# Prompt attention: the gathered value rows of the sample's sparse branch moved from the last tiles of sparse heads to the tiles ahead of them

## The reference, cut to what matters

```python
idx = indexer_topk(q_i, w_i, pos, ik_all, topk)
v_sel = gather_selected(pool_v.astype(v_b.dtype), page_table, v_b, idx, past_len)
dsa_o = dsa_attend(q_b, pos, k_sel, v_sel, idx)

def dsa_attend(q, q_pos, k_sel, v_sel, idx):
    ...
    p = jax.nn.softmax(s, axis=-1).astype(v_sel.dtype)
    o = jnp.einsum('bhqs,bqshd->bqhd', p, v_sel)
```

## Time and profile before

| what | before |
|---|---|
| median of 3 runs | 1791.02 us (1786.36 to 1791.84) |
| the profiled execution | 1787.65 us, span 1785.7 us |
| PE busy | 1640.2 us (92% of the span) |
| DVE busy | 867.5 us (49%) |
| ACT busy | 424.1 us (24%) |
| POOL busy | 345.0 us (19%) |

### The profile page before, as it was taken

How to read it: one execution, slowest core, us unless ns; L and a number is a source line. 1 busy time by engine, 2 the same in 40 slices (tenths; PEclk the granted TensorE clock), 3 DMA queues, 4 the chain that set the end, 5 groups by cost and what they waited for, 6 DMA issues and landing times.

```text
span 1785.7 us, 21665 instructions
## 1 busy us (share of the span) xinstructions
PE 1640.2 (92%) x8572; PEld 1008.0 (56%) x8572; DVE 867.5 (49%) x1636; ACT 424.1 (24%) x1111; POOL 345.0 (19%) x348
## 2 busy tenths in 40 slices
PE   6999989999989899977687699989999999989998
PEld 3644545447766666655453466535777777754443
DVE  3447897995805677774778633222222222210011
ACT  2132221010015455443355432001111111100000
POOL 2100000010006677761445520000000000000000
PEclk9899989999999899997788899999999999999999
DMA  8311221143217788776445744502212212112100
GB/s 259 131 48 63 100 76 61 68 183 112 92 67 254 267 284 261 270 235 194 138 131 151 240 140 155 153 0 80 73 48 71 71 48 77 65 36 71 63 23 31
DMA packets 89846, 218.38 MB, mean 122 GB/s; under 512 B 13576, under 2 KB 37520, under 8 KB 83696
## 3 DMA queue, kind: packets, MB, share of 16 engines
q0 software_dynamic: 29168, 116.66, 20.1%
q1 hardware_dynamic: 59506, 93.24, 15.8%
q10 hardware_dynamic: 1072, 7.09, 1.5%
HBM read 199.99 MB, written 16.84 MB: 121 GB/s over the span
## 4 chain that ended last, share of the span: by engine, by line
PE 82%; DVE 9%; issue 3%; ACT 2%; DMA 2%; POOL 1%; SPq 0%; ACTq 0%; DVEq 0%
PE PS L2062 13%; PE PS L630 13%; PE PS L2081 11%; PE PS L2064 7%; PE PS L681 7%; PE PS L740 5%; PE PS L2025 4%; PE PS L995 3%; PE PS L1044 3%; PE PS L1518 2%; DVE mem L1717 2%; PE PS L2002 2%; DVE mem L1716 2%; PE PS L1388 1%; PE PS L1002 1%
## 5 line engine op out<-in xcount | busy, mean ns | idle before, releaser
L2062 PE MATMUL PS<-mem 128*128 128x376 f32 x704 | 233.8, 485 | 0.0
L630 PE MATMUL PS<-mem 128*128 128x512 f32 (+3 forms) x580 | 232.4, 556 | 0.0
L2081 PE MATMUL PS<-mem 128*128 128x512 f32 (+1 forms) x440 | 191.0, 596 | 1.3 <-DVE mem L2257 1.3
L2062 PEld LDWEIGHTS PS<-mem 128*128 128x128 f32 x704 | 131.9, 190 | 80.0 <-issue 1.7
L630 PEld LDWEIGHTS PS<-mem 128*128 128x128 f32 (+1 forms) x580 | 99.5, 184 | 118.3 <-issue 118.1
L1805 POOL DMA_INDIRECT mem<-in_cache_dsa_k,mem x128 | 144.9, 1132 | 54.5 <-issue 35.0
L1805 POOL DMA_INDIRECT mem<-in_cache_dsa_v,mem x128 | 122.9, 960 | 166.8 <-PE PS L1500 129.0
L2081 PEld LDWEIGHTS PS<-mem 128*128 128x128 f32 (+1 forms) x440 | 80.2, 183 | 111.5 <-issue 109.9
L2064 PE MATMUL PS<-mem 128*128 128x216 f32 x704 | 135.9, 345 | 0.0
L2064 PEld LDWEIGHTS PS<-mem 128*128 128x128 f32 x704 | 129.3, 189 | 11.2
L2238 DVE TENSOR_SCALAR mem<-mem 128x528 f32<-128x528 f32 x22 | 12.2, 555 | 250.7 <-ACT mem L2144 250.7
(11 more groups left out here) (312 smaller groups left out, 2106.2 us busy)
## 6 DMA issues: line engine op xcount, KB each, us to landing
mem<-in_w_in SPq DMA_DIRECT2D x10, 2048.0 KB, 8.2
mem<-in_w_ffn_g SPq DMA_DIRECT2D x11, 1024.0 KB, 5.4
mem<-in_w_ffn_u SPq DMA_DIRECT2D x11, 1024.0 KB, 5.4
mem<-in_w_ffn_d SPq DMA_DIRECT2D x10, 1024.0 KB, 5.1
tmp_gates<-mem SPq DMA_DIRECT2D x16, 296.0 KB, 2.1
mem<-tmp_gates SPq DMA_DIRECT2D x16, 296.0 KB, 6.1
mem<-in_w_o SPq DMA_DIRECT2D x2, 2048.0 KB, 11.7
mem<-in_x_prompt SPq DMA_DIRECT2D x6, 512.0 KB, 13.1
```

Source lines behind the costliest of these rows:

```text
L630: ins = pe.matmul(PS[0:n, b[bank], out_at:out_at + width], left[:, k, cols], w[:, k, at:at + width], start=k == 0, stop=k == k_range - 1)
L2062: pe.matmul(PS[:, b + j, 0:UP_A], w[:, k, :], h2T[:, k, 0:UP_A], start=k == 0, stop=k == KD - 1)
L2081: return pe.matmul(PS[0:TW[m], (5 * n + m) % 8, :], upT[:, f, token_cols(m)], w[:, i, :], start=f == 0, stop=f == NF - 1)
```

## The change

It changes six entries of `v_cost`. The weights of the steps in the last three tiles of branch B fall from 5, 4 and 5 to 3, 1 and 1, that of tile 3 of A from 8 to 7, that of tile 0 of B rises from 3 to 4; the sum of all weights falls from 184 to 148, so that every other step's share grows.

```diff
-        v_cost = [{("a", 4): 0, ("b", 4): 4, ("a", 0): 6, ("b", 0): 3, ("a", 1): 6, ("b", 1): 5, ("a", 2): 7,
-                   ("b", 2): 4, ("a", 3): 8, ("b", 3): 5}[x[0:2]] for x in pairs_p]
+        v_cost = [{("a", 4): 0, ("b", 4): 4, ("a", 0): 6, ("b", 0): 4, ("a", 1): 6, ("b", 1): 3, ("a", 2): 7,
+                   ("b", 2): 1, ("a", 3): 7, ("b", 3): 1}[x[0:2]] for x in pairs_p]
```

## The result

| | before | after |
|---|---|---|
| median of 17 runs each | 1791.84 us (1777.34 to 1796.77, and one of 6126.64) | 1775.15 us (1768.41 to 1781.16) |
| ratio to before | | 0.9923, 95% interval 0.9907 to 0.994 |
| the profiled execution | 1787.65 us, span 1785.7 us | 1768.41 us, span 1766.5 us |

The change made the kernel faster by 0.77%, 13.8 us by the ratio (10.8 to 16.7 by its interval). The ratio is taken over the fast runs, without the one of 6126.64, and is not the quotient of the two medians (0.9907, 16.7 us).

A forecast was written before the change was run, and what follows sets the result against it. PE bounds the last eight steps, DVE the steps that pick top keys, where a row may be free. Eight terms sum to -9.9 us, counted from the three-run median of 1791.02: 1781 us, range 1773 to 1789.

The forecast's parts named there:

- 1 last eight steps: Steps 28 to 35: 13 rows become 4, so PE has less to do; -6.9 us (-4.5; -8).
- 2 wait for in_w_br_a: PE's wait for this load: fewer row gathers issued beside it shorten it; -3.4 us (0; -5.5).
- 3 step 8: No row waits there for ACT's copy of sums, so the next score starts earlier; -5.5 us (-2.5; -6.5).
- 4 steps 6 and 12: Rows coming later or in greater number fill part of PE's idle time; -1.8 us (+1; -4.5).
- 5 steps 3 and 5: New waits for ACT's copy of sums: step 3 may end late, step 5 free; +1.7 us (0; +3.5).
- 6 steps 14 and 15: New waits for ACT's copy of sums may make PE late for DVE; +2.0 us (0; +5.8).
- 7 step 18: Row 40 waits for ACT's copy of sums and delays the indexer scores; +4.3 us (+2.5; +5.4).
- 8 steps 20 to 23: Two new waits for ACT's copy of sums cost 1.5, step 22's goes; -0.3 us (-1.8; +4).
- A sign I had named as one of error: PE waits for gathered row values (rows_in, DMA) ahead of L1500 would show the forecast wrong.
- The other two signs of error: DVE waits of 3 us or more in steps 15, 16, 21, 22; a last stretch above 68 us.
- handovers cost more: Added waits for ACT's copy of sums cost 20.5 us, more than the rows were worth: 1798; chance 0.08.
- the last steps are not PE's alone: Last eight steps: the chain part, product, part shows once rows go, gain there only -3, 1785; chance 0.10.

The follow-up runs named there:

- e4: Kernel before with row 12 alone moved from step 8 to step 9: 1781.86 us, ratio to before 0.9956.
- e5: As e1, but rows 60 to 63 stand in steps 24 to 27 and the last eight steps hold none: 1764.33 us, ratio to before 0.9851.
- e8: Changed kernel with one more POOL wait, holding gathers of rows 60 to 63 until in_w_br_a has landed: 1771.69 us, ratio to before 0.9893.
- e3: Changed kernel with row 40 alone moved from step 18 to step 19: 1771.25 us, ratio to before 0.9895.
- e1: Changed kernel with rows per step rewritten so every group of four ends at a step's end: 1772.17 us, ratio to before 0.9902.
- e9: As e5, but with four rows in steps 4, 9, 14, 15, 16, 21, 22 and 23: 1770.61 us, ratio to before 0.9888.
- e6: Changed kernel run again without edit for a second profiled execution: 1777.12 us, ratio to before 0.992.
- e2: As e1, but all rows one place later, so a group's end falls inside 14 steps: 1797.14 us, ratio to before 1.0045.
- e7: Kernel before run again without edit for a second profiled execution: one execution, 1791.6 us.

## Why the prediction was right, and where its terms were off

1781 (1773 to 1789), faster, was forecast; 1775 came, inside the range and faster by more than 0.3%. The gain by the ratio is 13.8 where the sum gave 9.9, so the sum was short by 0.9 at the least (the interval ends at 10.8). Term by term, from the shifts:

| term | forecast | first profile | second profile |
|---|---|---|---|
| 1 last eight steps | -6.9 | -6.5 | -6.1 |
| 2 wait for in_w_br_a | -3.4 | -4.1 | -4.3 |
| 3 step 8 | -5.5 | -4.9 | -6.5 |
| 4 steps 6 and 12 | -1.8 | -4.2 | -1.7 |
| 5 steps 3 and 5 | +1.7 | 0.0 | +3.0 |
| 6 steps 14 and 15 | +2.0 | +1.3 | +2.7 |
| 7 step 18 | +4.3 | +2.4 | +3.2 |
| 8 steps 20 to 23 | -0.3 | -1.1 | -0.9 |

(From the table of shifts: term 5 is the one at step 6; 4 from 6 to 8 and 12 to 14; 3 from 8 to 12; 6 from 14 to 16; 7 from 18 to 20; 8 from 20 to 24; 2 from 24 to part; 1 from part to end.) In the mean of the two profiles terms 1, 3, 5 and 6 lie within 0.6 of the forecast, and 2, 4, 7 and 8 came out 0.7 to 1.5 better each.

- **Terms 1 and 3 held**, each within 1.0, and e4 and e5 show their causes. What rows cost in the last steps, and what a handover ahead of DVE's next mask costs, could be read from before.
- **Term 2 held in its mechanism**: nine gathers became four and e8 moves the load by holding more of them. Its size is less sure than the two values look: both count from the 9.3 of one execution of before; by PE's waits against the 7.1 of the other the term is -2.0 to -2.4.
- **Terms 5 and 6 were prices between two outcomes.** For term 5 both came: step 3 costs nothing at full clock and 2.9 at half, and I had 1.7. That the mean of two profiles lies near it is luck of two draws. Term 6 never saw its cheap end: behind step 14's handover the granted clock was 0.70 in the first profile of the change (919.8 to 924.7) and 0.50 in the second (925.4 to 930.3), and DVE stood 1.28 and 2.44 for the mask of step 15; in e3, whose first row there ran at full clock, it fell behind that row (0.65, 933.1 to 938.0), and DVE stood 1.51.
- **Term 7 was mis-sized**, by 1.5 in the mean. The delay of the first score itself was as worked out (4.98 more than before in the first profile, 5.17 in the second). But of it I gave back "about 1" for the clock, and 2.6 and 2.0 came back; of these 1.9 and 1.3 are two sets of indexer scores, which took 2.08 each before and 1.13 each in the first profile, 1.72 and 1.13 in the second.
- **Terms 4 and 8 were too careful**: step 12's indexer scores took 0.92 in place of 1.65 in both profiles of the change, since PE was at full clock there, and the masks won 2.3 to 2.4 from step 12 to 14. In e3, whose table is the same up to step 17, they took 1.43 and 1.65, and nothing was won: this gain too hangs on the clock of the execution. What step 6 gave differs as much (from step 6 to 8: -1.9 and +0.7). And the new handovers of steps 20 and 21 cost 0.9 together in both, not 1.5 (from step 20 to 22).
- **A sign I had named as one of error came true without harm**: a wait of 3.15 for gathers in step 17, whose mask of step 18 didn't move. DVE's pace covered it, as e1's waits. My count, by which the last rows land as they are wanted, was off there (e9). The other two signs of error stayed away: DVE's longest wait for the scores of steps 15, 16, 21 and 22 is 1.28, in e6 2.44, and the last stretch is 64.70.

The rival "handovers cost more" had the right mechanism but not the price: 1.8 each in e2, not 2.7. It is no empty threat: with handovers in 14 steps the kernel is slower than before. The rival "the last steps are not PE's alone" fell: in the change PE waits once for DVE's product, 0.21 in step 28.

The Trainium skill's rule (TensorE: Matmul & The Clock Gate, section HAM oscillation), that a gap in PE's work throttles the clock behind it, is borne out by e6 in step 3 (2.48, then 0.50) and not by the first profile of the change in the same place (2.49, then 1.00).

## What to carry to other kernels

Work that fills a slower engine's shadow is free only if it doesn't stop its own engine there: first move group boundaries to the ends of steps (one row moved out of step 8 gave 0.44%, one out of step 18 3.7 to 4.5 us by the masks), then move the rows. A wait behind which the clock is uncertain can only be priced between both outcomes, and one profile of either kernel is one draw: take a second before splitting a gain of 1% into terms. Work placed ahead of a load's wait pays twice, once for its own time and once because the engine doesn't stand (e5: the next piece took 2.80 in place of 5.38).

## What was not expected of the hardware

The same handover, with the same wait, is followed by either clock. The table gives the granted clock in the 5 us from the row behind the handover on (3 us in step 10); 1.00 is 2.4 GHz, 0.50 is 1.2 GHz, and what lies between had both. In the middle column that row still ran at full clock (its eight matmuls took 0.62 to 0.66) and the clock fell behind it; in the last column it ran at half from the row on (1.04; 0.76 in e3's step 3), and rose again where the value is 0.70.

| place, wait | full throughout | full, then half | half |
|---|---|---|---|
| step 3, 2.48 to 2.49 | change, e8: 1.00 | | e6 0.50; e3 0.54 |
| step 10, 1.75 to 1.76 | before, e7, e6, e8: 1.00 | change 0.66; e3 0.73 | e4 0.50 |
| step 14, 3.25 to 3.28 | | e3, e2 0.65 | change 0.70; e6, e8 0.50 |
| step 18, 2.27 to 2.28 | e2 1.00 | | change 0.70 |
| step 20, 3.42 | e6 1.00 | change 0.65; e8, e2 0.66 | e3 0.50 |

The stretch behind step 10's handover, in the change and in e6, which is the same kernel (columns of the earlier trace rows, PEclk the third from the end):

```profile
894.42:897.50 3.08, 3.08 (x32) 2.28 (x33) 2.02 (x9) 0.34 (x2) 2.25 (x3) 0.66 0.71 213
901.60:904.70 3.10, 3.10 (x36) 2.24 (x36) 2.16 (x10) 1.16 (x4) 2.28 (x3) 1.00 0.72 213
```

So the length of the wait alone doesn't tell the clock behind it. What else does is open: no run here varied it by itself. And the load of in_w_br_a, with nine gathers behind its issue each time, landed 15.9, 13.8 and 12.5 after it and made PE wait 9.3, 7.1 and 5.9 in three executions (before, e7, e4).
